# A decoder layer's first microseconds: activation table loaded ahead of the data, first weight and x tiles taken in halves, parameters on another queue, three products of ones first

## The reference

```python
def rmsnorm(x, g):
    y = xf * lax.rsqrt(jnp.mean(xf * xf, axis=-1, keepdims=True) + EPS)
    return (y * g).astype(x.dtype)

h = rmsnorm(x, g_mix[l])
(nq, nkc, nvc, nks, nvs, nkw, nvw, ngt, mq, mk, mv, mo, mi, mf) = split_cols(h @ w_in[l], IN_SIZES)
o_nsa = nsa_batched(...)                    # attention over compressed, selected and near keys
h_m = mlstm_chunkwise(...)                  # the other head group
x = x + mixed @ w_out[l]                    # then memory attention, gated MLP, final RMSNorm
```

## Time and profile before

| | |
|---|---|
| median of 3 runs | 1655.78 us (1655.39 to 1655.97) |
| span of the profiled execution, first to last instruction | 1653.0 us |
| PE busy in the span | 1617.6 us (98%) |
| DVE, ACT, POOL busy | 1204.2, 725.1, 873.2 us |
| first matmul of the product | 10.06 us |
| first of the sums of squares on PE | 34.66 us |

### The profile page before, as it was taken

One profiled execution on the slowest core, in us unless ns is written; L12 is line 12 of the kernel. 1 busy time (PEld: TensorE's weight loads), 2 busy tenths in 40 slices (PEclk: granted clock), 3 DMA queues, 4 the chain that ended last, 5 costly groups with the idle time before them and its releaser, 6 DMA issues.

```text
span 1653.0 us, 22437 instructions
## 1 busy us (share of the span) xinstructions
PE 1617.6 (98%) x8126; PEld 1346.8 (81%) x8126; DVE 1204.2 (73%) x1599; ACT 725.1 (44%) x1389; POOL 873.2 (53%) x676
## 2 busy tenths in 40 slices
PE   7998999999999999999999999999999999999997
PEld 6887888887888888898888878778888888887886
DVE  6765888887788875464555457788887887888955
ACT  5114888885322342253233134344444444533444
POOL 3233555454333334303226343599988878789841
PEclk9999999999999999999999999999999999999999
DMA  5130201110111132242100431345434444874522
GB/s 195 60 131 27 65 27 39 37 42 27 52 64 39 50 117 102 101 154 90 39 26 28 151 115 38 131 166 178 175 134 141 140 145 167 304 282 140 167 82 102
DMA packets 80426, 176.46 MB, mean 107 GB/s; under 512 B 7932, under 2 KB 24508, under 8 KB 80192
## 3 DMA queue, kind: packets, MB, share of 16 engines
q1 hardware_dynamic: 68040, 135.71, 24.1%
q10 hardware_dynamic: 12280, 39.34, 6.3%
HBM read 136.21 MB, written 38.81 MB: 106 GB/s over the span
## 4 chain that ended last, share of the span: by engine, by line
PE 61%; DVE 17%; POOL 10%; ACT 6%; issue 6%; DMA 1%; ACTq 0%; POOLq 0%; DVEq 0%; SPq 0%
PE ps L1104 14%; PE ps L1108 14%; PE ps L1107 14%; DVE x_t L3036 4%; PE ps L1305 4%; POOL sum_s L1015 3%; ACT x_t L2219 2%; PE ps L1327 2%; POOL w_lo L1009 2%; PE ps L1328 2%; DVE x_t L3065 2%; POOL s_new L1035 1%; DVE ps L3028 1%; ACT w_hi L2206 1%; PE ps L1268 1%
## 5 line engine op out<-in xcount | busy, mean ns | idle before, releaser
L1104 PE MATMUL ps<-h_hi,w_hi 128*128 128x512 f32 x1060 | 418.3, 395 | 3.9 <-ACT p_sum L2188 2.3
L1108 PE MATMUL ps<-h_hi,w_lo 128*128 128x512 f32 x1060 | 413.0, 390 | 0.0
L1107 PE MATMUL ps<-h_lo,w_hi 128*128 128x512 f32 x1060 | 412.9, 390 | 0.0
L913 POOL TENSOR_TENSOR w_hi<-w_raw,ones 128x1024 fp32r<-128x1024 f32 x51 | 103.3, 2025 | 493.8 <-PE ps L1104 471.7
L1104 PEld LDWEIGHTS ps<-h_hi,w_hi 128*128 128x128 f32 x1060 | 199.0, 188 | 52.5 <-ACT p_sum L2188 8.7
L1108 PEld LDWEIGHTS ps<-h_hi,w_lo 128*128 128x128 f32 x1060 | 199.0, 188 | 42.3
L1107 PEld LDWEIGHTS ps<-h_lo,w_hi 128*128 128x128 f32 x1060 | 199.2, 188 | 38.5
L952 POOL TENSOR_SCALAR probs<-probs,nsa_inv,gate_sig 128x640 f32<-128x640 f32 (+7 forms) x128 | 100.8, 788 | 128.5 <-DVE nsa_inv L2608 128.3
L3036 DVE SCALAR_TENSOR_TENSOR x_t<-ps,par,x_t 128x1023 f32<-128x1023 f32 x84 | 107.7, 1282 | 72.7 <-ACT x_t L2219 71.2
L918 POOL TENSOR_TENSOR w_lo<-w_raw,w_hi 128x1024 fp32r<-128x1024 f32 x51 | 136.5, 2676 | 3.9
L2391 DVE TENSOR_TENSOR pt_lo<-ps,pt_hi 128x512 fp32r<-128x512 f32 (+6 forms) x148 | 100.4, 683 | 11.9 <-ACT pt_hi L1903 10.2
(11 more groups left out here) (415 smaller groups left out, 4027.1 us busy)
## 6 DMA issues: line engine op xcount, KB each, us to landing
w_raw<-in_w_tiles SPq DMA_DIRECT2D x109, 512.0 KB, 3.3
w_raw<-in_w_tiles SPq DMA_DIRECT2D x55, 256.0 KB, 3.2
s_new<-in_w_tiles SPq DMA_DIRECT2D x44, 256.0 KB, 4.0
z_dram<-x_t ACTq DMA_DIRECT2D x21, 512.0 KB, 2.9
b<-z_dram SPq DMA_DIRECT2D x33, 256.0 KB, 3.6
q_st<-q_dram SPq DMA_DIRECT2D x64, 128.0 KB, 2.9
x_dram<-x_t ACTq DMA_DIRECT2D x14, 512.0 KB, 2.8
t_dram<-t_new ACTq DMA_DIRECT2D x22, 256.0 KB, 5.1
```

Of the source, the lines that this page charges most:

```text
L913: pool.tensor_tensor(w_hi[s][:, :], w_raw[s][:, :], ones[:, :].to_broadcast([P, KT * P]), ALU.mult).then_inc(w_hi_made.sem, w_hi_made.up())
L1104: ins = mm(out_ap, whi, x_hi, start=first, stop=False)
L1107: mm(out_ap, whi, x_lo, start=False, stop=False)
L1108: return mm(out_ap, wlo, x_hi, start=False, stop=last)
```

## The change

Five things at the start of the program, all before 35 us:

1. ACT issues the DMA of the parameters itself, and then does one activation of a single column of ones, into `table_junk`. ACT's table load stands ahead of it and no longer waits for data. The wait for the parameters moves behind the first half of wf 0.
2. `wf_raw0` and `wf_raw1` come in two halves of 512 columns (row tiles 0 to 3, and 4 to 7 of the contraction). SP's order is wf 0 first half, x 0, wf 1 first half, x 1 to 3, wf 0 and wf 1 second halves, x 4 to 7. `first_high` and `first_low` of the second halves come in ACT's and DVE's order after the square and the addition of k = 1, and PE waits for them at k = 4.
3. x 0 and x 1 are still loaded whole, but ACT and DVE split each in two instructions of 512 tokens, and PE waits for each token half by itself. x_split therefore ends at 10 and not at 8, for POOL too.
4. DVE's first instruction fills half of `r_in` with ones.
5. PE does three products of these ones (128x512, float32 and not fp32r) into an otherwise unused bank, before it waits for masks and data.

```diff
--- before.py
+++ after.py
@@ -373,6 +373,7 @@
         mmask = keep("mmask", [P, P])
         ident_r = keep("ident_r", [P, P], FP32R)
         col_r = keep("col_r", [P, 2, TT], FP32R)
+        table_junk = keep("table_junk", [P, 1])
         FREE = cursor[0]
 
 
@@ -645,18 +646,22 @@
                 sp.dma_start(w_raw[s][:, :], w_tiles[n].rearrange("a p m -> p (a m)") if not isinstance(n, int)
                              else w_tiles[FIRST + n, :, :]).then_inc(loaded[s].sem, loaded[s].up())
 
-            def load_first(z):
-                sp.dma_start(wf_raw[z][:, :], w_tiles[z, :, :]).then_inc(t(f"wf_loaded{z}", 16).sem, 16)
+            def load_first(z, part):
+                loaded_part = t((f"wf_loaded{z}", f"block_loaded{KT + z}")[part], 16)
+                cs = slice(part * HALF, part * HALF + HALF)
+                sp.dma_start(wf_raw[z][:, cs], w_tiles[z, :, cs]).then_inc(loaded_part.sem, loaded_part.up())
 
             def load_x(k):
                 sp.dma_start(x_f[:, k, :], x_rows[k, :, :]).then_inc(t(f"block_loaded{k}", 16).sem, 16)
 
-            sp.dma_start(par[:, :], params[:, :]).then_inc(t("gains_loaded", 16).sem, 16)
-            load_first(0)
+            load_first(0, 0)
             load_x(0)
-            load_x(1)
-            load_first(1)
-            for k in range(2, KT):
+            load_first(1, 0)
+            for k in range(1, 4):
+                load_x(k)
+            for z in range(FIRST):
+                load_first(z, 1)
+            for k in range(4, KT):
                 load_x(k)
             sp.dma_start(w1[:, :, :, :], cmp_first.rearrange("p (a l h) -> p a l h", a=2, l=CMP_STRIDE)).then_inc(
                 t("small_loaded", 16).sem, t("small_loaded", 16).up())
@@ -931,7 +936,7 @@
 
             assert FIRST_KV % 2 and TILES % 2
             x_split = t("x_split")
-            x_split.add(KT)
+            x_split.add(KT + 2)
             pool.wait_ge(x_split.sem, x_split.value())
             split_tile(0)
             split_pairs(4)
@@ -984,7 +989,7 @@
             piece_high, piece_split = t("piece_high"), t("piece_split")
-                piece_high.n = FIRST
+                piece_high.n = 2 * FIRST
...
@@ -1147,6 +1152,9 @@
                 last.then_inc(chunk_done.sem, chunk_done.up())
 
 
+            pe.wait_ge(t("vector_chain").sem, 1)
+            for _ in range(3):
+                mm(ps[:, 7, :], r_in[:, 0:P], r_in[:, 0:HALF], start=True, stop=True)
             masks_ready.add(3)
             pe.wait_ge(masks_ready.sem, masks_ready.value())
             def token_sums(squares, bank, at_col=0):
@@ -1177,12 +1185,15 @@
 
 
             for k in range(KT):
-                pe.wait_ge(x_split.sem, x_split.next())
+                if k >= 2:
+                    pe.wait_ge(x_split.sem, x_split.next())
                 for z in range(FIRST):
-                    if k == 0:
+                    if k % 4 == 0:
                         pe.wait_ge(piece_split.sem, piece_split.next())
                     w = (wf_hi[z][:, k * P:k * P + P], wf_lo[z][:, k * P:k * P + P])
                     for c in range(2):
+                        if k < 2 and z == 0:
+                            pe.wait_ge(x_split.sem, x_split.next())
                         cs = slice(c * HALF, c * HALF + HALF)
                         last = product(ps[:, 2 * z + c, :], w, h_hi[:, k, cs], h_lo[:, k, cs], k == 0, k == KT - 1)
                         if k == KT - 1:
@@ -1780,16 +1791,20 @@
                     std_ready.sem, std_ready.up())
 
             gains_loaded = t("gains_loaded", 16)
-            gains_loaded.add(1)
-            act.wait_ge(gains_loaded.sem, gains_loaded.value())
-
-            def first_high(z):
-                act.wait_ge(t(f"wf_loaded{z}", 16).sem, t(f"wf_loaded{z}", 16).next())
-                f(wf_hi[z][:, :], wf_raw[z][:, :], ACT.Copy).then_inc(t("piece_high").sem, t("piece_high").up())
-
-            def x_high(k):
-                act.wait_ge(t(f"block_loaded{k}", 16).sem, t(f"block_loaded{k}", 16).next())
-                f(h_hi[:, k, :], x_f[:, k, :], ACT.Copy, scale=gains[:, G_MIX, k:k + 1]).then_inc(
+            act.dma_start(par[:, :], params[:, :]).then_inc(gains_loaded.sem, gains_loaded.up())
+            act.wait_ge(t("vector_chain").sem, 1)
+            f(table_junk[:, :], r_in[:, 0:1], ACT.Copy).then_inc(junk_written.sem, junk_written.up())
+
+            def first_high(z, part):
+                loaded_part = t((f"wf_loaded{z}", f"block_loaded{KT + z}")[part], 16)
+                act.wait_ge(loaded_part.sem, 16)
+                cs = slice(part * HALF, part * HALF + HALF)
+                f(wf_hi[z][:, cs], wf_raw[z][:, cs], ACT.Copy).then_inc(t("piece_high").sem, t("piece_high").up())
+
+            def x_high(k, cs=slice(0, SEQ)):
+                if cs.start == 0:
+                    act.wait_ge(t(f"block_loaded{k}", 16).sem, t(f"block_loaded{k}", 16).next())
+                f(h_hi[:, k, cs], x_f[:, k, cs], ACT.Copy, scale=gains[:, G_MIX, k:k + 1]).then_inc(
                     hi_ready.sem, hi_ready.up())
 
             def x_square(k):
@@ -1798,14 +1813,20 @@
                 sq_used.add(1)
 
             sq_used.add(2)
-            first_high(0)
-            x_high(0)
-            x_high(1)
-            first_high(1)
+            first_high(0, 0)
+            act.wait_ge(gains_loaded.sem, gains_loaded.value())
+            for cs in (slice(0, HALF), slice(HALF, SEQ)):
+                x_high(0, cs)
+            first_high(1, 0)
+            for cs in (slice(0, HALF), slice(HALF, SEQ)):
+                x_high(1, cs)
             for k in range(KT):
                 x_square(k)
                 if k + 2 < KT:
                     x_high(k + 2)
+                if k == 1:
+                    for z in range(FIRST):
+                        first_high(z, 1)
             norm_root()
 
             def high_keys(br):
@@ -2421,29 +2442,36 @@
                     vector_chain.sem, vector_chain.up())
                 dve.wait_ge(vector_chain.sem, vector_chain.value())
 
+            dve.memset(r_in[:, 0:HALF], 1.0).then_inc(vector_chain.sem, vector_chain.up())
             clear_sums(acc_x)
             for z in (kc_a, vc_hl):
                 dve.memset(whole(z).bitcast(FP32), 0.0).then_inc(vector_chain.sem, vector_chain.up())
             t("gains_loaded", 16).add(1)
             dve.wait_ge(t("gains_loaded", 16).sem, t("gains_loaded", 16).value())
 
-            def first_low(z):
+            def first_low(z, part):
                 dve.wait_ge(t("piece_high").sem, t("piece_high").next())
-                low(wf_lo[z][:, :], wf_raw[z][:, :], wf_hi[z][:, :]).then_inc(t("piece_split").sem, t("piece_split").up())
-
-            def x_low(k):
+                cs = slice(part * HALF, part * HALF + HALF)
+                low(wf_lo[z][:, cs], wf_raw[z][:, cs], wf_hi[z][:, cs]).then_inc(t("piece_split").sem, t("piece_split").up())
+
+            def x_low(k, cs=slice(0, SEQ)):
                 wait_hi()
-                low(h_lo[:, k, :], x_f[:, k, :], h_hi[:, k, :], gains[:, G_MIX, k:k + 1]).then_inc(
+                low(h_lo[:, k, cs], x_f[:, k, cs], h_hi[:, k, cs], gains[:, G_MIX, k:k + 1]).then_inc(
                     x_split.sem, x_split.up())
 
-            first_low(0)
-            x_low(0)
-            x_low(1)
-            first_low(1)
+            first_low(0, 0)
+            for cs in (slice(0, HALF), slice(HALF, SEQ)):
+                x_low(0, cs)
+            first_low(1, 0)
+            for cs in (slice(0, HALF), slice(HALF, SEQ)):
+                x_low(1, cs)
             for k in range(KT):
                 if k + 2 < KT:
                     x_low(k + 2)
                 add_square(k % 2, acc_x, sq_x)
+                if k == 1:
+                    for z in range(FIRST):
+                        first_low(z, 1)
             columns_start(6)
             columns_end()
             copy_spread(r_in[:, :], 6)
...
```

More of the change, by code:

```diff
@@ L1552, in _ @@
             out_slot, piece_split = [], t("piece_split")
-            piece_split.n = FIRST
+            piece_split.n = 2 * FIRST
             def first_outputs(z, c, k0, k1):
@@ L2256, in down_highs @@
                     block_loaded = t(f"block_loaded{k}", 16)
-                    block_loaded.n = {0: 1, 1: 2, 3: 3, 5: 5, 6: 4}[n] + (k < KT)
+                    block_loaded.n = {0: 1, 1: 2, 3: 3, 5: 5, 6: 4}[n] + (k < KT + FIRST)
                     act.wait_ge(block_loaded.sem, block_loaded.value())
@@ L3109, in z_sum @@
                 block_loaded = t(f"block_loaded{k}", 16)
-                block_loaded.n = (3 if n == 2 else 4) + (k < KT)
+                block_loaded.n = (3 if n == 2 else 4) + (k < KT + FIRST)
                 dve.wait_ge(block_loaded.sem, block_loaded.value())
```

## The result

| | before | after |
|---|---|---|
| median of the device time | 1655.78 us (1654.97 to 1656.42) | 1661.3 us (1659.95 to 1662.7) |
| time of the profiled execution | not shown | 1660.15 us |
| its span | 1653.0 us | 1658.4 us |

The ratio is 1.0034, 95% interval 1.0023 to 1.0044: the change makes the kernel 5.5 us slower. Forecast was 1654.6, with a range of 1653.6 to 1657.5, and 4% for slower by over 0.2%. The forecast was wrong, and the range too.

A forecast was written before the change was run, and what follows sets the result against it. PE's queue bounds the kernel, but DVE's additions hold its sums. Of 5.9 us PE gains, 3.4 to 3.5 go in the new wait and about 1.2 in small waits; 1.2 remain: 1654.6 us, range 1653.6 to 1657.5.

The forecast's parts named there:

- Start: PE's start: first real product at 6.9 instead of 10.06, 3.2 us, plus up to 2.7 us from warming with ones.
- Rival 2: PE's first products: ones don't warm the array, yet sums start at the same moment; 1654.6 us, chance 0.1 within the forecast's.
- Second halves: DVE's row: x_low 2 starts 1.05 us earlier, two half low parts add 1.2; x_low 7 ends 0.15 us later.
- early bound: DVE's x_low 2 if x 1 lands at 7.6: starts at 11.1, additions end at 32.5.
- Tail: DVE's three additions beside POOL's weight split: kept at 7.3 us after the last x_low, before and after.
- Rival 3: Additions after x_low 7: another DVE and POOL order ends them at 29.8; 4.6 us gained, 1651.2 us, chance 0.04.
- New wait: PE before the sums: through at 30.0, idle about 3.4 us for the additions, sums at 33.5 instead of 34.66.
- small waits for DVE: PE's early products at k = 1, 2 and 4: about 1.2 us of its gain lost waiting.
- Rival 1: Sums and products behind: clock falls in PE's 3.4 us wait; 1656.1 to 1657.5 us, middle 1656.8, chance 0.42.
- Behind them all is as before: Everything after the sums: unchanged, since weights and roots are released by the same events.
- Median against span: Whole program: the median stands 2.8 us above the profiled span, turning span 1651.8 into 1654.6.

The follow-up runs named there:

- a_acthigh: Changed kernel without moved tiles or products of ones, ACT instead of POOL making the first general weight tile's high part: 1653.5 against 1656.11 us for the kernel before.
- a_mid: a_acthigh with the sums of squares placed after the first twelve products of the general tile: 1654.18 against 1655.91 us for the kernel before.
- a_noones_mid: Changed kernel without moved tiles or ones, POOL making both weight parts, sums after the general tile's first twelve products: 1654.47 us, 0.9993 of the kernel before.
- a_shift64: Changed kernel with the junk tile 64 bytes long instead of 4, so tiles move by 64 bytes: 1661.38 us, 1.0033 of the kernel before.
- b_shift32: Kernel before plus one unused 4-byte tile ahead of FREE, later tiles 32 bytes higher, no instruction changed: 1660.1 against 1656.14 us.
- a_noshift: Changed kernel without the added table_junk tile, the table-loading activation writing a column overwritten later: 1658.24 against 1656.14 us for the kernel before.

## Why the prediction was wrong

Step by step, as it put them:

- **Start.** The ones ran from 1.53, as said, until 7.0 (forecast 4.2 to 6.9: they ran at the lower clock to the end). First real product 7.64 (6.9): ACT's half of x 0 begins at 5.99, so x 0 landed near 5.9 and not at 5.5, and 0.2 us lie between DVE's end and PE. Spacing 0.23 from the first product: right. Rival 2 fell.
- **Second halves.** Two half low parts in DVE's row: 16.00 to 17.21, 1.21 us (1.2). x_low 2 at 11.33 (11.9, early bound 11.1). x 1 did land earlier than before, which was the bound and not the value taken; this term of the early part was mis-sized, by 0.6 us.
- **Tail.** 7.36 us (7.3). Right, and Rival 3 fell; a_acthigh then shortened it by giving POOL less, as its reason wants.
- **New wait.** PE's last early product starts at 29.87 (through at 30.3); it waits 2.54 us (3.4), and the sums are at 32.81 (33.5, bound 32.5). That PE is through near the forecast 30.0 is luck: it started 0.7 us late, its 96 products took 0.6 us more because of the tile, and the 1.2 us of small waits for DVE did not come. 1.85 us were gained here against before's profile, not 1.2, and 0.9 to 2.7 against its four copies. The reading that DVE's additions set the end, and that an earlier PE mostly waits longer, held.
- **Rival 1** (0.42) came true. The clock fell, from 34.76 to 38.18 by the record of granted clock, and 1.7 us went. It fell also in the profiles of all the kernels in which PE waited ahead of the sums (0.22 to 2.97 us; seven of them), and in none of the seven in which the sums had no wait in front (before, its four copies with moved tiles, a_mid and a_noones_mid). That is one execution of each. In its own terms the prediction placed the point of decision between 1.6 and 3.1 us of idle time; a_acthigh's clock fell with 0.22, and 1.4 us after the dense products had begun again. It looked at idle time alone, and not at the 1.8 us of one-column products that follow. These are not always needed: in a_shift64 the clock fell at 32.4, in the wait itself, 2.0 us behind the last 128x512 product. The rule of the Trainium skill, TensorE: Matmul & The Clock Gate, section "HAM oscillation — how this bites in real kernels", that the prediction quoted, for matmuls that wait between groups, gave the right outcome, though the waits in its example are longer than the 2.54 us here; that a wait of 0.22 us with one-column products behind it can go before a fall, the rows of a_acthigh show.
- **"Behind them all is as before"** is the step that failed, and it is the larger half of the miss. The prediction costed every instruction that the diff moves and not the one tile that it adds. b_shift32 (4.0 us) and a_noshift (3.4 us) measure that tile's price from two sides. From the pairs alone it would be 1008 x 6 ns = 6.0 us. Some of it seems to be swallowed where PE waited anyway: in front of the products of z PE was idle for 0.9 us (with w_hi) and 1.1 us (with spare) before, and for 0.0 and 0.5 us after.
- **Median against span.** The 2.8 us between them were read as what lies around the span. All other profiles say 1.7 to 1.8; the rest was a profiled execution without the second fall. This alone would have shifted the forecast by nothing, since before and after were both held against the median, but it makes the difference of the two spans 1.0 us too large.

**The sum, put right.** The tile costs 3.4 to 4.0 us. The rest is 2.1 us (a_noshift): the early gain of 1.85, less one or two stretches at the lower clock. In a_noshift's profile the low stretch lasts 6.8 us, and its copy of the roots starts at 45.45, 1.57 us later than in before's profile (0.7 to 2.5 later than in its four copies), which could be most of the 2.1; the kernel after had only 3.4 us of it in its own profile, so this part is argued and not shown. Together 5.5 to 6.1 us, measured 5.5 (3.8 to 7.3); the lower end is exact by its making, the upper one is independent of it.

Without the tile's 3.4 to 4.0 us the time would have been 1657.3 to 1657.9, at the upper edge of the range.

## What to carry to other kernels

Before a new scratch tile is allocated in front of others, see what it moves: put it last, or pad it to 256 bytes, and compare the mean ns of the same instruction by pair of tiles, since a few ns on a thousand products show in no wait. An engine that sits on nearly all of the time gains nothing from an early start as long as another engine's chain ends in front of it; shorten that chain (here by taking one of two POOL instructions out of DVE's way), or put other work ahead of the join. And a stretch of tiny matmuls behind even a short wait is a place to look for a fall of the clock. One profile shows one execution: a fall in it need not be in most of them, and a start of PE's early stage differs by up to 1.8 us between profiles of the same queue.

## What the runs showed of the hardware

- **Distance of the operands.** A 128x512 product of 4-byte values costs 0.227 us from start to start in the kernel before, where its weights and its moving tile start at the same place modulo 256 bytes, and 0.233 in most pairs with 32, 64 or 128 bytes more between them (with 64, one pair did not change and another hardly); 256 more, or 32 for both, change nothing. The Trainium skill, SBUF — State Buffer, section "Who interferes with whom", gives PE two read ports, one for the moving tile and one for weight loads, and calls them independent. The 6 ns that b_shift32 adds to a product speak against full independence, though what meets, and where, no run here shows.
- **The clock falls at or behind tiny products with almost no idle time.** In the kernel after, PE works from 121.86 to 126.7 without a gap, on transposes and products of 4 to 128 columns, waits 0.25 us, and runs at 1.2 GHz from 126.9 to 130.3, at a price of 1.6 us (1.41 + 0.16 in the table above). The same stretch of 3.4 us stands in thirteen of fourteen profiles, beginning at 123.8 to 129.6; in a_noones_mid it begins among the small products. The profile of before has the same row of products and the same 0.25 us, and its clock stays up. It is part of the kernel before, and nothing here tried to mend it.
